# The silu of the MLP's gate goes to the gate's PSUM banks, and the product reads it there

## The chip, the cores and the metric

The kernel runs on one core of a Trainium2 chip. The metric is the device time of one execution in microseconds (us), the median over the runs. Engines are named as in the profile: PE is TensorE (PEld its weight loads), DVE is VectorE, ACT is ScalarE, POOL is GpSimd, SP is the queue that issues most transfers.

## The reference

One layer of a hybrid decoder on 1024 tokens of width 1024, in float32. After a mixer of three head groups comes the gated MLP, and the change lies in its first half:

```python
def conv_gated_mlp(x, w_up, conv_w, w_down):
    h = causal_dwconv(x @ w_up, conv_w)       # 3 taps over the tokens, per channel
    gt, val = jnp.split(h, 2, axis=-1)        # 2 x 2816 channels
    return (jax.nn.silu(gt) * val) @ w_down
```

## The kernel before

The up stage works on 22 tiles j of 128 gate channels and the 128 value channels that belong to them; tokens lie along the free axis, 1024 columns of float32. Each weight and each activation is split in a high and a low half (`slab_p`, `slab_q`; the high one on ScalarE, L2080, the low one on GpSimd, L2087, in a ring of five), and both are multiplied.

Tiles 0 to 2 are done in the plain way, 3 and 4 in four groups of matmuls (A1, A2, B1, B2), and 5 to 21 in seven products of half size, a scheme of Strassen's kind. Each of the seven is a group of eight matmuls (L2263) named by a number i. TensorE's order is 5, 6, 2, 7 of tile j, 1 of tile j+1, then 4 and 3 of tile j. The groups need sums of weights, which VectorE makes ahead (`weight_sum`, L2210; "s" in the written order), copies of some products in SBUF (`copied`, ScalarE, L2144; "k"), and adds of these copies to other products in PSUM (`added`, VectorE, L2217; "a").

A tile's gate and value take two PSUM banks each (`c_ps(0, j)` and `c_ps(1, j)`), and tiles of the same parity share their four banks. When a tile's products are complete, ScalarE writes the convolution's last tap from PSUM to an SBUF buffer (`tapped`, L2102; "t"), and VectorE adds the two other taps to it, reading PSUM again (`tap_one`, L2165, "c"; `tap_zero`, L2171, "v"). For the gate, g = 0, the buffer is `y_a`, one for all tiles; for the value, g = 1, it is `y_b[j % 2]`. ScalarE applies silu to `y_a` in place (L2136; "y"), and VectorE multiplies `y_a` into `y_b` (`prod`, L2227; "p"). The product goes out to memory (`spill`) and is read back in the down stage.

TensorE's groups 5 and 2 write the gate's banks and wait, before the change, for the gate's last tap of tile j-2 (`conv_done(pe, 0, j - 2)`); group 1 waits for that of the value.

All engines follow one order written out by hand, `UP_ORDER` (L298 to L328): each takes from it the steps that are its own. A part of it, for three tiles:

```
... a2.11 s5.12 k7.11 v0.10 h5.12 l5.12 a5.11 y10 s6.12 h2.12 s7.12 k1.12 l2.12 h6.12 p10 h7.12 l6.12 t1.11 a3.11 ...
... a2.14 s5.15 k7.14 a5.14 h5.15 v0.13 l5.15 h2.15 k1.15 s6.15 l2.15 y13 s7.15 h6.15 t1.14 p13 l6.15 h7.15 a3.14 ...
... a2.18 k7.18 s5.19 a5.18 h5.19 v0.17 h2.19 l5.19 k1.19 s6.19 y17 l2.19 s7.19 h6.19 t1.18 l6.19 a3.18 p17 ...
```

"p13" is the product of tile 13, "v0.13" the last tap of its gate, "s6.15" the weight sum of group 6 of tile 15, "h" and "l" the high and low halves of a group's weights. VectorE's own steps are a, s, v, c and p.

Of the kernel before, what the change touches and what calls it, by code (L numbers as in the profile page):

```python
# [25 lines left out]
ACT = mybir.ActivationFunctionType  # L26
ALU = mybir.AluOpType
# [24 lines left out]
NF = DFF // P  # L52
# [220 lines left out]
CLASSIC = 3  # L273
# [141 lines left out]
def build(nc, a, out, scratch, qkv_mid, act_mid, decay_mid, tri_mid, inv_mid, invt_mid):  # L415
    ctx = ExitStack()
    with ctx:
# [7 lines left out]
        def late(name, value=0):  # L425

            early, base = LATE[name]
            return sem(early), base + value
# [315 lines left out]
        y_a = R.view(19456, [S])  # L744
        y_b = [R.view(w, [S]) for w in (27648, 26624)]
        c_ps = lambda g, j: psum[:, 4 * (j % 2) + 2 - 2 * g:4 * (j % 2) + 4 - 2 * g, :].rearrange("p a b -> p (a b)")
# [1222 lines left out]
        def prod_done(eng, j):  # L1969
            eng.wait_ge(*late("up_prod", PRODS.index((j,)) + 1))  # L1970
# [4 lines left out]
        def conv_done(eng, g, j):  # L1975
            eng.wait_ge(*late("up_conv", CONVS.index((g, j)) + 1))
# [112 lines left out]
        def y_of(g, j):  # L2089
            if j < CLASSIC:  # L2090
                return act_f[j] if g else y_up[(j + 1) % 2]
            return y_b[j % 2] if g else y_a

        def conv_source(g, j):
            return up_ps[j % 2][:, g] if j < CLASSIC else c_ps(g, j)

        def up_act(act):
            for s in range(2):
                act.wait_ge(sem(f"x1_st{s}"), 16 * NT // 2)

            def tapped(g, j):
                act.activation(y_of(g, j), conv_source(g, j), ACT.Copy, scale=tap(2, 2 * j + g)).then_inc(late("up_tap")[0], 1)  # L2102

            def tap_(g, j):
                if j < CLASSIC:
                    act.wait_ge(*late("up_mm", 2 * j + g + 1))
                elif j in SEVEN:
                    for i in ((2, 3), (5,))[g]:
                        add_done(act, i, j)
                    mult_done(act, (3, 4)[g], j)  # L2110
                else:
                    mult_done(act, (A2, B2)[g], j)
                if g == 0 and (j == 2 or j >= CLASSIC):
                    prod_done(act, j - 1 if j >= CLASSIC else j - 2)
                elif g == 1 and j >= CLASSIC + 2:
                    spilled(act, j - 2)
                elif g == 1 and j >= CLASSIC:
                    t_ready(act, 7)
                    t_ready(act, 4)
                tapped(g, j)  # L2120

            def t_hi(i):
                t_made(act, "S", i)
                if i == 6:
                    act.wait_ge(*late("up_mm", 1))
                if i == 7:
                    t_ready(act, 4)
                    t_ready(act, 6)
                if i == 4:
                    act.wait_ge(*late("up_mm", 2 * CLASSIC))  # L2130
                    prod_done(act, 1)
                act.activation(t_p[i], t_f[i], ACT.Copy, scale=SPLIT_W).then_inc(late("t_hi")[0], 1)

            def silu(j):
                conv_done(act, 0, j)
                act.activation(y_of(0, j), y_of(0, j), ACT.Silu).then_inc(late("up_silu")[0], 1)  # L2136

            def copied(i, j):

                mult_done(act, i, j)  # L2140
                before = max((x for x in SEVEN if x < j), default=None)
                if before is not None:
                    add_done(act, {1: 2, 6: 3, 7: 5}[i], before)
                act.activation(u_s[i], mult_ps(i, j), ACT.Copy).then_inc(late("c_cp")[0], 1)  # L2144

            up_run(dict(U=lambda u: up_split_hi(act, u), h=lambda i, j: split_mult_hi(act, i, j), k=copied, t=tap_, y=silu, H=t_hi,
                        f=lambda kk: dn_split_hi(act, kk), i=lambda kk: act_split_hi(act, kk)))

# [11 lines left out]
        def up_dve(v):  # L2160

            def tap_one(g, j):
                u, c, y = 2 * j + g, conv_source(g, j), y_of(g, j)
                v.wait_ge(*late("up_tap", TAPS_UP.index((g, j)) + 1))
                v.scalar_tensor_tensor(out=y[:, 1:S], in0=c[:, 0:S - 1], scalar=tap(1, u), in1=y[:, 1:S],  # L2165
                                       op0=ALU.mult, op1=ALU.add).then_inc(late("up_c1")[0], 1)

            def tap_zero(g, j):
                u, c, y = 2 * j + g, conv_source(g, j), y_of(g, j)
                v.wait_ge(*late("up_c1", TAPS_ONE.index((g, j)) + 1))  # L2170
                v.scalar_tensor_tensor(out=y[:, 2:S], in0=c[:, 0:S - 2], scalar=tap(0, u), in1=y[:, 2:S],  # L2171
                                       op0=ALU.mult, op1=ALU.add).then_inc(late("up_conv")[0], 1)

            T_FROM = {5: (0, 0), 7: (0, 1), 6: (1, 1), 4: (1, 0)}

            def whole(i):
                if i in (6, 4):
                    v.wait_ge(*late("up_mm", 2))
                v.scalar_tensor_tensor(out=t_f[i], in0=x_quad(h2_p, *T_FROM[i]), scalar=1.0 / SPLIT_W - 1.0, in1=x_quad(h2_q, *T_FROM[i]),
                                       op0=ALU.mult, op1=ALU.add).then_inc(late("t_f")[0], 1)  # L2180

            def t_sum(i):
                x, y = {5: (7, 5), 7: (6, 7), 6: (6, 5), 4: (4, 6)}[i]
                for z in (x, y):
                    t_made(v, "W", z)
                if i != 5:
                    t_made(v, "S", {7: 5, 6: 7, 4: 6}[i])
                v.tensor_tensor(t_f[i], t_f[x], t_f[y], ALU.subtract).then_inc(late("t_f")[0], 1)

            def t_lo(i):  # L2190
                v.wait_ge(*late("t_hi", T_HIS.index((i,)) + 1))
                v.scalar_tensor_tensor(out=t_q[i], in0=t_p[i], scalar=1.0 - 1.0 / SPLIT_W, in1=t_f[i], op0=ALU.mult, op1=ALU.add)                    .then_inc(late("t_lo")[0], 1)

            def weight_sum(i, j):
                if i == 5:
                    pair_landed(v, j)
                    if seven_before(j) is not None:
                        part_done(v, 3, seven_before(j))
                    out, x, y, op = s_e1[j % 2], w_of(j, 1, 0), w_of(j, 1, 1), ALU.add
                elif i == 6:  # L2200
                    sum_done(v, 5, j)
                    out, x, y, op = s_e2[j % 2], s_e1[j % 2], w_of(j, 0, 0), ALU.subtract
                elif i == 7:
                    sum_done(v, 5, j)
                    out, x, y, op = w_of(j, 1, 0), w_of(j, 0, 0), w_of(j, 1, 0), ALU.subtract
                else:
                    sum_done(v, 6, j)
                    part_done(v, 5, j)
                    out, x, y, op = s_e1[j % 2], w_of(j, 0, 1), s_e2[j % 2], ALU.subtract
                v.tensor_tensor(out, x, y, op).then_inc(late("s_add")[0], 1)  # L2210

            def added(i, j):

                mult_done(v, i, j)
                copy_done(v, {2: 1, 5: 7, 3: 6}[i], j)
                out = c_ps(1, j)[:, right] if i == 5 else mult_ps(i, j)
                v.tensor_tensor(out, mult_ps(i, j), u_s[{2: 1, 5: 7, 3: 6}[i]], ALU.add).then_inc(late("c_add")[0], 1)  # L2217

            def prod(j):
                if j < CLASSIC:  # L2220
                    return
                if j == CLASSIC:
                    for x in range(CLASSIC):
                        prod_done(v, x)
                v.wait_ge(*late("up_silu", SILUS.index((j,)) + 1))
                conv_done(v, 1, j)
                v.tensor_tensor(y_b[j % 2], y_a, y_b[j % 2], ALU.mult).then_inc(late("up_prod")[0], 1)  # L2227

            v.wait_ge(*late("wo_mm", NT))
            v.wait_ge(*late("v_tp", NT))  # L2230
            for s in range(2):
                v.wait_ge(sem(f"x1_st{s}"), 16 * NT // 2)
            v.wait_ge(*late("v_lo", NT))
            up_run(dict(W=whole, S=t_sum, T=t_lo, s=weight_sum, a=added, c=tap_one, v=tap_zero, p=prod, j=lambda kk: act_split_lo(v, kk)))

        def up_pe(pe):
# [7 lines left out]
            for n, (i, j) in enumerate(MULTS):  # L2244
# [1 line left out]
                if i in (1, B1):  # L2246
                    conv_done(pe, 1, j - 2)
                if i in (2, 5, A1):
                    conv_done(pe, 0, j - 2)
                if j < CLASSIC + 2 and i in (1, 2, 5, A1, B1):  # L2250
                    conv_done(pe, 1, j - 2)
                if i in t_p:
# [879 lines left out]
```

## Time and profile before

| what | us |
|---|---|
| median of 3 runs | 1063.14 |
| lowest and highest run | 1062.17, 1066.04 |
| span of the profiled execution | 1063.3 |
| TensorE busy in it | 1025.7 (96%) |
| VectorE busy in it | 813.6 (77%) |
| ScalarE busy in it | 635.0 (60%) |
| GpSimd busy in it | 501.6 (47%) |

The span runs from the first to the last instruction of the profiled execution; it lies 0.2 us above the median of the timed runs. The up stage's groups of seven run from 673.3 to about 892 us of it, the down stage from there to the end. The granted TensorE clock is 1.00 of full speed through both, but for the very end.

### The profile page before, as it was taken

Reading aid. Unit: us, or ns where it says so; the run is one execution under the profiler, and the core shown is the slowest. Engines: PE = TensorE matmul, PEld = TensorE weight load, DVE = VectorE, ACT = ScalarE, POOL = GpSimd, SP = SyncE. Lnnn points to the kernel's source line nnn. Section 1 sums busy time; section 2 is a strip of 40 time slices with the busy share of each in tenths; the row PEclk is TensorE's granted clock in tenths of the full one; section 3 lists DMA queues with packets and bytes.
Section 4 is the critical chain, followed back from the end, with each engine's and each line's share of the span. In section 5 each row is a group of like instructions: output and inputs, shape, how many; then the busy total and the mean of one; then the engine's idle time right before and its main releaser. Section 6 shows DMA issues by size and latency. Waiting matters only on the chain.

```text
span 1063.3 us, 19006 instructions
## 1 busy us (share of the span) xinstructions
PE 1025.7 (96%) x7090; PEld 833.7 (78%) x7090; DVE 813.6 (77%) x1140; ACT 635.0 (60%) x1201; POOL 501.6 (47%) x653
## 2 busy tenths in 40 slices
PE   4999999998999999999999999999999998999997
PEld 4978878986777778777688787888887786888885
DVE  5798895755667886877577598899899999656755
ACT  6634423347777766777865454666666667546443
POOL 2356424725453654542320277788788886000000
PEclk9999999996999999999999999999999999999999
DMA  9245311352122122112263612233443335955961
GB/s 276 68 119 178 110 57 27 70 125 58 41 60 59 27 53 49 29 30 60 80 209 136 198 53 80 79 119 122 127 127 123 123 115 192 382 178 180 334 239 79
DMA packets 159522, 126.77 MB, mean 119 GB/s; under 512 B 63908, under 2 KB 137928, under 8 KB 159432
## 3 DMA queue, kind: packets, MB, share of 16 engines
q1 hardware_dynamic: 157992, 120.32, 37.7%
q10 hardware_dynamic: 1440, 5.24, 1.2%
q8 instruction: 57, 0.93, 0.4%
q14 instruction: 33, 0.27, 0.1%
HBM read 99.79 MB, written 25.71 MB: 118 GB/s over the span
## 4 chain that ended last, share of the span: by engine, by line
PE 60%; DVE 7%; POOL 4%; ACT 3%; issue 3%; DMA 0%; DVEq 0%; ACTq 0%; POOLq 0%
PE psum L2475 14%; PE psum L2263 12%; PE psum L1771 5%; PE psum L1720 5%; PE psum L1704 4%; POOL slab_q L2087 4%; PE psum L1546 4%; PE psum L1689 3%; PE psum L1886 3%; PE psum L2269 2%; DVE arena L2171 1%; DVE arena L2165 1%; PE psum L1625 1%; PE psum L1605 1%; ACT arena L1219 1%
## 5 line engine op out<-in xcount | busy, mean ns | idle before, releaser
L2087 POOL TENSOR_TENSOR slab_q<-arena,slab_p 128x512 fp32r<-128x512 f32 x127 | 208.2, 1667 | 45.5 <-ACT slab_p L2080 45.4
L2475 PE MATMUL psum<-dn_p,ap_p 128*128 128x512 f32 x352 | 110.2, 392 | 2.7 <-DVE arena L2171 1.4
L2475 PE MATMUL psum<-dn_q,ap_q 128*128 128x512 f32 x352 | 109.7, 391 | 0.0
L2263 PE MATMUL psum<-t_p,slab_p 128*128 128x512 f32 x272 | 106.3, 391 | 1.3 <-ACT arena L2144 0.8
L2263 PE MATMUL psum<-t_q,slab_q 128*128 128x512 f32 x272 | 105.9, 389 | 0.0
L2080 ACT ACTIVATE slab_p<-arena 128x512 fp32r<-128x512 f32 x127 | 78.2, 627 | 38.7 <-PE psum L2263 13.9
L2301 DVE TENSOR_TENSOR dn_q<-arena,dn_p 128x1024 fp32r<-128x1024 f32 x41 | 50.2, 1224 | 56.3 <-ACT dn_p L2291 56.0
L1431 DVE CUSTOM_DVE_ANT_0 psum<-psum,arena 128x640 f32<-128x640 f32 (+7 forms) x96 | 67.7, 718 | 31.2 <-PE psum L1689 30.6
L2291 ACT ACTIVATE dn_p<-arena 128x1024 fp32r<-128x1024 f32 x44 | 46.6, 1058 | 70.0 <-PE psum L2475 63.6
L3051 PE MATMUL psum<-h_p,cm_p 128*128 128x512 f32 (+1 forms) x288 | 87.5, 375 | 0.6 <-DVE arena L2958 0.6
L3051 PE MATMUL psum<-h_q,cm_q 128*128 128x512 f32 (+1 forms) x288 | 86.9, 373 | 0.0
L2263 PE MATMUL psum<-h_p,slab_p 128*128 128x512 f32 x204 | 79.9, 391 | 0.7 <-POOL slab_q L2087 0.7
L2475 PEld LDWEIGHTS psum<-dn_p,ap_p 128*128 128x128 f32 x352 | 65.7, 188 | 18.8 <-issue 2.5
L1219 ACT ACTIVATE arena<-psum,arena 128x640 f32<-128x640 f32 (+7 forms) x96 | 67.1, 702 | 21.1 <-DVE arena L1431 20.3
L2263 PE MATMUL psum<-h_q,slab_q 128*128 128x512 f32 x204 | 79.4, 389 | 0.0
L2466 POOL TENSOR_TENSOR arena<-arena 128x1024 f32<-128x1024 f32 x1 | 2.4, 2352 | 160.6 <-DVE arena L2439 160.6
L2475 PEld LDWEIGHTS psum<-dn_q,ap_q 128*128 128x128 f32 x352 | 66.1, 188 | 14.5
L2936 DVE SCALAR_TENSOR_TENSOR arena<-psum,arena 128x1023 f32<-128x1023 f32 (+29 forms) x60 | 75.9, 1265 | 1.4
L1226 ACT ACTIVATE arena<-psum 128x384 f32<-128x384 f32 x132 | 60.1, 488 | 23.3 <-PE psum L1704 22.1
L2210 DVE TENSOR_TENSOR arena<-arena 128x512 f32<-128x512 f32 x68 | 72.6, 1082 | 0.0
L2576 POOL TENSOR_TENSOR cm_q<-arena,cm_p 128x1024 fp32r<-128x1024 f32 x16 | 39.2, 2449 | 61.8 <-ACT cm_p L2571 61.7
L1720 PE MATMUL psum<-arena 128*64 128x192 f32 x528 | 64.2, 348 | 1.4 <-ACT arena L1226 1.4
(319 smaller groups left out, 2636.4 us busy)
## 6 DMA issues: line engine op xcount, KB each, us to landing
arena<-in_ffn_w_up SPq DMA_DIRECT2D x44, 512.0 KB, 4.9
arena<-in_ffn_w_down SPq DMA_DIRECT2D x44, 512.0 KB, 3.9
arena<-in_w_in SPq DMA_DIRECT2D x20, 512.0 KB, 3.9
act_mid<-arena SPq DMA_DIRECT2D x18, 512.0 KB, 2.6
arena<-act_mid SPq DMA_DIRECT2D x36, 256.0 KB, 4.7
arena<-in_x SPq DMA_DIRECT2D x16, 512.0 KB, 4.6
qkv_mid<-arena ACTq DMA_DIRECT2D x9, 512.0 KB
arena<-qkv_mid SPq DMA_DIRECT2D x8, 576.0 KB, 4.9
```

The costliest lines, as they stand in the source:

```text
L1219: act.activation(probs(u), s_psum(u, n), ACT.Exp, scale=-1.0, bias=nmx[:, u % 2:u % 2 + 1], accum_out=psums[:, NH * kind + h:NH * kind + h ...
L1226: act.activation(pt[x % 2].rearrange("p g c -> p (g c)"), psum[:, bank, 0:GDIM], ACT.Copy).then_inc(done, 1)
L1431: v.tensor_tensor_reduce(out=s_psum(u, n), in0=s_psum(u, n), in1=hidden, scale=-1.0, scalar=-NEG, op0=ALU.add, op1=ALU.min, accum_out=nmx[ ...
L1720: ins = pe.matmul(psum[tok, 7, 0:GDIM // 2], val[:, b, kind, HD * kv:HD * (kv + 1)], pt[x % 2][:, :, tok], start=b == k0, stop=True, skip_ ...
L1771: ins = pe.matmul(wm_ps[WM_SLOT[t]][:, n * 512:(n + 1) * 512], x[:, k], w[:, n * 512:(n + 1) * 512], start=first and k == ks[0] and w is w ...
L2080: act.activation(slab_p[n % RING], part_source(i, j), ACT.Copy, scale=1.0 - SPLIT_W).then_inc(late("up_hi")[0], 1)
L2087: pool.tensor_tensor(slab_q[n % RING], part_source(i, j), slab_p[n % RING], ALU.subtract).then_inc(late("up_lo")[0], 1)
L2210: v.tensor_tensor(out, x, y, op).then_inc(late("s_add")[0], 1)
L2263: ins = pe.matmul(mult_ps(i, j), w[:, k], x[:, k], start=k == 0 and x is x_p[i] and i in (1, 2, 5), stop=True, skip_group_check=True)
L2475: ins = pe.matmul(dn_ps[t % HT][:, n * 512:(n + 1) * 512], x[:, tok], w[:, n * 512:(n + 1) * 512], start=first and x is ap_p[s], stop=True ...
L2936: own.up(v.scalar_tensor_tensor(out=cacc[:, c, s:S], in0=glu[c][:, 0:S - s], scalar=w, in1=cacc[:, c, s:S], op0=ALU.mult, op1=ALU.add))
L3051: ins = pe.matmul(cm_ps[i % 2][:, c0:c1], w[:, k], x[:, k, c0:c1], start=k == 0 and x is h_p, stop=True, skip_group_check=True)
```

## The change

For tiles 3 to 19 silu is written to the gate's PSUM banks, whose sums have been read for the last time by then; the product takes its first operand there. `y_a` is then free as soon as silu has read it, so ScalarE's next tap into it waits for silu instead of the product. The gate's banks are free only when the product has read them, so TensorE's groups 5 and 2 of tile j wait for the product of tile j-2. Tiles 20 and 21 keep silu in `y_a`. `UP_ORDER` is as before.

```diff
+        def gate_of(j):
+            return c_ps(0, j) if CLASSIC <= j < NF - 2 else y_of(0, j)
+        def silu_done(eng, j):
+            eng.wait_ge(*late("up_silu", SILUS.index((j,)) + 1))
+        def bank_free(eng, j):
+            if CLASSIC <= j < NF - 2:
+                prod_done(eng, j)
+            else:
+                conv_done(eng, 0, j)
...
-                if g == 0 and (j == 2 or j >= CLASSIC):
+                if g == 0 and CLASSIC < j < NF - 1:
+                    silu_done(act, j - 1)
+                elif g == 0 and (j == 2 or j >= CLASSIC):
                     prod_done(act, j - 1 if j >= CLASSIC else j - 2)
...
             def silu(j):
                 conv_done(act, 0, j)
-                act.activation(y_of(0, j), y_of(0, j), ACT.Silu).then_inc(late("up_silu")[0], 1)
+                act.activation(gate_of(j), y_of(0, j), ACT.Silu).then_inc(late("up_silu")[0], 1)
...
-                v.tensor_tensor(y_b[j % 2], y_a, y_b[j % 2], ALU.mult).then_inc(late("up_prod")[0], 1)
+                v.tensor_tensor(y_b[j % 2], gate_of(j), y_b[j % 2], ALU.mult).then_inc(late("up_prod")[0], 1)
...
                 if i in (2, 5, A1):
-                    conv_done(pe, 0, j - 2)
+                    bank_free(pe, j - 2)
```

CLASSIC is 3 and NF is 22.

## Rows read from the trace of the kernel before

**Rows 1.** The page: each engine's busy time, share of the span, instructions.

```profile
PE 1025.7 (96%) x7090; PEld 833.7 (78%) x7090; DVE 813.6 (77%) x1140; ACT 635.0 (60%) x1201; POOL 501.6 (47%) x653
```

**Rows 2.** Stretches: length, busy time of each engine, granted clock, DMA share, GB/s.

```profile
core 0: us, PE busy (x) PEld busy (x) DVE busy (x) ACT busy (x) POOL busy (x), PEclk, DMA share, GB/s
...
762.50:853.90 91.40, 90.46 (x393) 73.07 (x393) 91.25 (x84) 61.34 (x92) 76.91 (x50) 1.00 0.39 121
```

**Rows 3.** Waits from 640 to 905 us: total, times, longest.

```profile
PEld psum L2263 <- POOL slab_q L2087: 4.5, 9, 0.6
```

**Rows 4.** Timeline of TensorE: start and length in us, first matmuls of groups.

```profile
673.30 0.39 PE L2263 MATMUL psum<-t_p,slab_p 128*128 128x512 f32 x1
...
685.99 0.39 PE L2263 MATMUL psum<-t_p,slab_p 128*128 128x512 f32 x1
...
788.55 0.39 PE L2263 MATMUL psum<-t_p,slab_p 128*128 128x512 f32 x1
...
795.80 0.44 PE L2263 MATMUL psum<-h_p,slab_p 128*128 128x512 f32 x1
...
801.31 0.39 PE L2263 MATMUL psum<-t_p,slab_p 128*128 128x512 f32 x1
...
853.90 0.39 PE L2263 MATMUL psum<-t_p,slab_p 128*128 128x512 f32 x1
```

**Rows 5.** Timeline of VectorE: start and length in us, idle time before in brackets.

```profile
672.84 1.28 DVE L2165 SCALAR_TENSOR_TENSOR arena<-psum,arena 128x1023 f32<-128x1023 f32 x1 [2.94 <-ACT arena L2102]
674.04 1.75 DVE L2227 TENSOR_TENSOR arena<-arena 128x1024 f32<-128x1024 f32 x1
...
683.51 2.31 DVE L2227 TENSOR_TENSOR arena<-arena 128x1024 f32<-128x1024 f32 x1
...
787.98 2.31 DVE L2227 TENSOR_TENSOR arena<-arena 128x1024 f32<-128x1024 f32 x1
...
796.75 0.69 DVE L2217 TENSOR_TENSOR psum<-psum,arena 128x512 f32<-128x512 f32 x1
797.35 1.27 DVE L2171 SCALAR_TENSOR_TENSOR arena<-psum,arena 128x1022 f32<-128x1022 f32 x1
798.54 2.64 DVE L2210 TENSOR_TENSOR arena<-arena 128x512 f32<-128x512 f32 x2
801.10 2.33 DVE L2227 TENSOR_TENSOR arena<-arena 128x1024 f32<-128x1024 f32 x1
...
854.11 0.70 DVE L2217 TENSOR_TENSOR psum<-psum,arena 128x512 f32<-128x512 f32 x1 [0.35 <-PE psum L2263]
854.71 1.28 DVE L2227 TENSOR_TENSOR arena<-arena 128x1024 f32<-128x1024 f32 x1
```

**Rows 6.** Single lines of VectorE: durations min/median/max in ns, first and last start.

```profile
L2227 DVE TENSOR_TENSOR arena<-arena x19: 1209/1746/2328, 674.0 to 900.4; 128x1024 f32<-128x1024 f32 x19
L2210 DVE TENSOR_TENSOR arena<-arena x68: 671/934/1842, 662.2 to 883.5; 128x512 f32<-128x512 f32 x68
L2165 DVE SCALAR_TENSOR_TENSOR arena<-psum,arena x44: 1266/1271/1285, 613.6 to 896.6; 128x1023 f32<-128x1023 f32 x44
L2217 DVE TENSOR_TENSOR psum<-psum,arena x51: 680/686/700, 679.4 to 893.5; 128x512 f32<-128x512 f32 x51
```

**Rows 7.** Timeline at the start of the down stage: VectorE, then TensorE.

```profile
895.44 1.28 DVE L2171 SCALAR_TENSOR_TENSOR arena<-psum,arena 128x1022 f32<-128x1022 f32 x1
...
896.87 0.70 PE L2475 MATMUL psum<-dn_p,ap_p 128*128 128x512 f32 x2 [1.02 <-DVE arena L2171]
```

**Rows 8.** Timeline of ScalarE: the copy of group 7 and silu in one tile.

```profile
796.00 0.60 ACT L2144 ACTIVATE arena<-psum 128x512 f32<-128x512 f32 x1 [2.03 <-PE psum L2263]
...
798.89 1.05 ACT L2136 ACTIVATE arena<-arena 128x1024 f32<-128x1024 f32 x1
```

**Rows 9.** Groups of ScalarE by form: busy us, mean ns of one.

```profile
L2792 ACT ACTIVATE psum<-psum 128x1024 f32<-128x1024 f32 x2 | 2.0, 1008 | 4.5 <-PE psum L3051 4.5
```

**Rows 10.** Stretches of the down stage, columns as in the second group.

```profile
891.70:920.00 28.30, 25.96 (x110) 20.16 (x109) 19.98 (x20) 13.21 (x16) 4.17 (x2) 1.00 0.89 329
920.00:960.00 40.00, 40.00 (x176) 32.83 (x175) 21.42 (x24) 18.97 (x24) 0.00 (x0) 1.00 0.68 240
```

## The prediction

> **What bounds the kernel now.** I read the page first. TensorE is busy in nearly the whole span, VectorE in three quarters of it [rows 1]; that is an average over stages, so the next view is the table of stretches around the change. In the middle of the up stage, from 762.5 to 853.9 us, TensorE has work 90.46 of 91.40 us and VectorE 91.25 of 91.40 [rows 2]. Two engines are full there at once, and VectorE is the one without reserve. The table of waits says what this costs TensorE: 4.5 us in nine waits for GpSimd's low halves, in which the longest is 0.6 us [rows 3].
>
> TensorE's own pace comes from the timeline. Call group (i, j) the eight matmuls of product i of tile j; the order is 5, 6, 2, 7, then 1 of the next tile, 4, 3. Group (5,14) starts at 788.55 and group (1,15), four groups later, at 795.80 [rows 4]: 1.81 us a group, 12.69 us for seven. From (5,5) at 673.30 to (5,19) at 853.90 are 14 tiles in 180.60 us [rows 4]; at 12.69 they would take 177.66. All waiting in that stretch is 2.9 us. This is the most that any relief of the other engines can give back there.
>
> **The change part by part.** *The new gate.* Group (5, j) overwrites the gate's right half of tile j-2. It used to wait for the last convolution tap of that gate; now it waits for the product of tile j-2, for j from 5 to 21: 17 gates. Group (2, j) gets the same wait and finds it met, since it comes two groups later. Behind (5, j) stands the whole TensorE queue, so each late product is a hole in the bounding engine. The question is where the product ends against the start of (5, j), which the VectorE timeline tells [rows 5].
>
> *The product itself.* Now it takes 1.21 to 2.33 us, median 1.75, for one and the same shape [rows 6]. What varies with it is the other instruction with both operands in SBUF, the weight sums at 671 to 1842 ns; instructions with one operand in PSUM keep one duration: the tap at 1266 to 1285 ns over 44, the add of half the length at 680 to 700 over 51 [rows 6], while GpSimd works beside them. The product with its gate in PSUM is of this second kind, so I take 1.23 us (twice the add less one fixed part: the bounds are its own 1.21 and the tap's 1.28, and 2.33 if the place of the operand did not matter; the nearest rows speak for the low end). Its end reaches TensorE after 0.15 us: a convolution ends at 895.44 + 1.28 = 896.72 and the matmul that waited for it starts at 896.87 [rows 7]. So a gate opens 1.38 us after the product starts.
>
> The Trainium skill ("VectorE: DVE Perf Modes", section on the TRN2 errata) speaks a little against this: it gives VectorE 62 cycles more for a PSUM source than for SBUF, by its 0.96 GHz an estimated 65 ns. The trace agrees in sign and not in size: the fastest SBUF sum of 512 columns takes 671 ns, the PSUM add 680 to 700 [rows 6]. By the page the stalls below would total about 0.5 us more.
>
> *First gate, (5,5).* The product of tile 3 starts at 674.04 behind a tap that waited for ScalarE until 672.84 [rows 5]; that tap needs tile 4's last group, so the order can't move. It opens at 675.42, group (5,5) started at 673.30 [rows 4]: a hole of 2.1 us.
>
> *Gates (5,6) to (5,11).* Here the product ends before the group begins. The tightest of the six is (5,6): the product ran from 683.51 for 2.31 us, to 685.82 [rows 5], and the group began at 685.99 [rows 4]; with 1.23 us it opens 1.1 us ahead. Nothing.
>
> *Gates (5,12) to (5,18).* These are the tiles in which VectorE never rests. For (5,14) the product starts at 787.98 [rows 5], opens at 789.36, the group started at 788.55 [rows 4]: 0.8 us. For (5,15): 801.10 and 802.48 against 801.31: 1.2 us. Of the seven, three have VectorE's order of (5,14) (0.8, 0, 0.8) and four that of (5,15) (1.2 each): 6.3 us if everything ahead of the product stays as it is. It does stay for a part: the chain from group 7 is paced by TensorE. Group 7 ends about 795.8, ScalarE's copy runs 796.00 to 796.60 [rows 8], the add at 796.75 is 8.20 us behind the start of (5,14), then the last tap, the two sums (2.64 us together) and the product [rows 5]. Relief of VectorE earlier in the tile cannot move that. What can move is the contention of the two sums: at 0.67 each the product would start at 8.20 + 0.60 + 1.19 + 1.2 = 11.2 us, but silu ends at 798.89 + 1.05 = 799.94, which is 11.39 [rows 8], so the gate opens at 12.8 us against 12.69: a hole of 0.1, and 0.6 us for all seven. Between 0.6 and 6.3 I take 4.0, nearer to the contended end, since the high half that ScalarE makes next after the copy sets GpSimd to work in just that part of the tile.
>
> *Gates (5,19) to (5,21).* In the written order the add of group 3 now stands ahead of the product (a3.18 p17, and so on). Group 3 of tile j-1 is the one right before (5, j) on TensorE. So the product cannot start before TensorE has run dry: the add started at 854.11, 0.21 behind (5,19), the product at 854.71 [rows 5], it would open at 856.09 against 853.90 [rows 4]. That is 2.2 us, three times: 6.6.
>
> *What is given back.* Holes let GpSimd fill its five slabs, and VectorE has up to 1.1 us less per tile: the 2.9 us of waits go, all but a little; I take 2.7.
>
> *The rest costs nothing.* Silu into PSUM: it takes 1.05 us from SBUF to SBUF [rows 8], and the one ScalarE instruction that writes 1024 columns of PSUM takes 1008 ns [rows 9]; ScalarE idles two fifths of the span, and uncovered it would cost the 0.1 us once per late gate at most. The gate's first tap on ScalarE waits for silu instead of the product: earlier, and not on TensorE's path. The last two tiles keep the old places, so the down stage's banks come free as before. Nor does it absorb the delay: it begins with 25.96 busy of 28.30 us, then 40.00 of 40.00 [rows 10], so at most some 2 us of its first waits could.
>
> The sum: 2.1 + 4.0 + 6.6 - 2.7 = +10.0 us on the profiled span of 1063.3, which is 0.2 above the median of the runs, 1063.14. So 1073 us; with 0.6 or 6.3 in the middle and 2.9 or 1.5 given back, 1069.5 to 1076.6.
>
> **The rivals.**
> *VectorE's relief decides (not slower).* VectorE paces tiles 10 to 16, at (853.90 - 801.31)/4 = 13.15 us a tile [rows 4]; 1.1 us less per product lets TensorE run at 12.69, and the product lands ahead of its gate. All holes away, it is 1063.3 - 2.9 = 1060.4. The point from which it decides: the product must start 11.3 us after (5, j-1). For: six gates already do so. Against: silu's end at 11.39, and the order at the last three. If only the middle holes vanish it is +5.8 or so, at the edge of what can be told; with some of it absorbed in the down stage it is within the noise.
>
> *The sums get worse.* GpSimd and the two sums block one another in turn: at 1.84 us each [rows 6] the product opens 2.4 us late four times and 1.2 us three times, 12.9 instead of 4.0: 1082. For: TensorE's holes shift GpSimd's work against VectorE's. Against: only a few sums reach that now. The Trainium skill ("SBUF — State Buffer", section Who interferes with whom) says that who starts first holds the shared port for the whole instruction, which would make this chance of phase all or nothing; the spread in [rows 6] agrees, and no run here shows which phase will come.
>
> *The product is no faster.* If the operand's place doesn't matter it keeps 2.33: 2.6 for the first gate, 1.1 more at each of seven, 3.3 at each of three; 2.6 + 11.7 + 9.9 - 2.7 gives 1085. Against it stand 95 PSUM instructions of one duration.
>
> **How the numbers follow.** A measurement of this kernel tells about 0.5%, 5.3 us, from no change. The forecast of +6 to +14 gets 0.68; worse sums 0.12; a product no faster 0.05; relief that eats most of the holes 0.15, of which 0.12 lies within 0.5% and 0.03 below it. So slower 0.85, same 0.12, faster 0.03. The range 1066 to 1080 leaves out the lower part of the relief case, the upper part of the worse sums and the product no faster: under 2 in 10.
>
> **What the profile would show.** Right: the product at 1.21 to 1.29 us throughout; TensorE waiting for VectorE's product line ahead of group 5, about 2.1 us at the first of these tiles and in the last three, under 1.3 in between, none in tiles 6 to 11; the waits for GpSimd's slabs nearly gone; VectorE with idle time between 762 and 854. Wrong: product durations still between 1.2 and 2.3; no wait ahead of (5,19) to (5,21); holes in tiles 6 to 11 too (contention moved there), or a down stage that starts 10 us later and ends less than 8 us later.

## The result and the profile after

The changed kernel takes 1081.17 us in the median (1079.93 to 1083.26, four runs) against 1063.33 beside it: 1.0165 times as long, with a 95% interval of 1.0149 to 1.0182, or 17.8 us. The forecast was slower, by 10; the range ended at 1080.

First the page of the changed kernel, each engine's busy time, as [rows 1].

```profile
PE 1029.1 (95%) x7090; PEld 834.5 (77%) x7090; DVE 799.4 (74%) x1140; ACT 633.7 (59%) x1201; POOL 479.0 (44%) x653
```

VectorE and GpSimd are busy for less time than before, and the kernel is slower. The stretch of [rows 2] shows the same in the middle of the up stage: VectorE was full and now rests 8.3 of 91.4 us; TensorE rested 0.9 and now rests 4.6.

```profile
core 0: us, PE busy (x) PEld busy (x) DVE busy (x) ACT busy (x) POOL busy (x), PEclk, DMA share, GB/s
762.50:853.90 91.40, 86.79 (x377) 69.80 (x376) 83.10 (x81) 56.28 (x86) 65.24 (x48) 1.00 0.37 116
```

The lines of the product, of silu and of the weight sums in the changed kernel, durations as in [rows 6] (L2243 was L2227, L2152 was L2136, L2226 was L2210):

```profile
L2243 DVE TENSOR_TENSOR arena<-psum,arena x17: 1208/1214/1218, 673.5 to 893.5; 128x1024 f32<-128x1024 f32 x17
...
L2152 ACT ACTIVATE psum<-arena x17: 1010/1022/1024, 668.1 to 890.3; 128x1024 f32<-128x1024 f32 x17
L2152 ACT ACTIVATE arena<-arena x5: 1043/1059/1066, 622.5 to 916.0; 128x1024 f32<-128x1024 f32 x5
...
L2226 DVE TENSOR_TENSOR arena<-arena x68: 678/746/1793, 661.7 to 895.8; 128x512 f32<-128x512 f32 x68
```

The 17 products with an operand in PSUM all take 1.21 us, where the same work took up to 2.33; silu is 0.04 us shorter into PSUM than into SBUF. Both instructions got cheaper, and the weight sums too in the median (746 ns against 934).

Why the product got shorter can be read beside GpSimd's timeline. The first two lines are of the kernel before, around its product of 801.10 to 803.43 us [rows 5]; the other two of the changed kernel, around a product of 845.01 to 846.22:

```profile
800.60 1.75 POOL L2087 TENSOR_TENSOR slab_q<-arena,slab_p 128x512 fp32r<-128x512 f32 x1
802.31 2.27 POOL L2087 TENSOR_TENSOR slab_q<-arena,slab_p 128x512 fp32r<-128x512 f32 x1
...
844.67 1.56 POOL L2087 TENSOR_TENSOR slab_q<-arena,slab_p 128x512 fp32r<-128x512 f32 x1
846.20 1.29 POOL L2087 TENSOR_TENSOR slab_q<-arena,slab_p 128x512 fp32r<-128x512 f32 x1
```

With both operands in SBUF the product ended 1.08 us behind the GpSimd instruction that was running when it began, and the next GpSimd instruction ended 1.15 us behind the product: they went one after the other. All nine products of 2.31 to 2.33 us before began beside a running GpSimd instruction like this; the eight of 1.21 to 1.28 began with GpSimd idle or within 0.2 us of the start or end of one of its instructions. With one operand in PSUM they run side by side: the product of 845.01 takes its 1.21 us beside a running GpSimd instruction, and one that began with the product of 748.39 took 1.31 us, where before one that began with the product of 747.13 took 2.36.

What the change cost stands in TensorE's timeline, ahead of group 5: of tile 5, of tile 18 and of tile 19 here.

```profile
670.97 0.39 PE L2279 MATMUL psum<-h_p,slab_p 128*128 128x512 f32 x1
...
672.56 0.39 PE L2279 MATMUL psum<-h_q,slab_q 128*128 128x512 f32 x1
674.84 0.47 PE L2279 MATMUL psum<-t_p,slab_p 128*128 128x512 f32 x1 [1.89 <-POOL slab_q L2087]
...
845.21 0.39 PE L2279 MATMUL psum<-h_q,slab_q 128*128 128x512 f32 x1
846.32 0.47 PE L2279 MATMUL psum<-t_p,slab_p 128*128 128x512 f32 x1 [0.72 <-POOL slab_q L2087]
...
858.88 0.39 PE L2279 MATMUL psum<-h_q,slab_q 128*128 128x512 f32 x1
861.23 0.47 PE L2279 MATMUL psum<-t_p,slab_p 128*128 128x512 f32 x1 [1.96 <-POOL slab_q L2087]
861.54 0.39 PE L2279 MATMUL psum<-t_q,slab_q 128*128 128x512 f32 x1
...
862.24 0.63 PE L2279 MATMUL psum<-t_p,slab_p 128*128 128x512 f32 x1
862.66 0.63 PE L2279 MATMUL psum<-t_q,slab_q 128*128 128x512 f32 x1
...
908.25 0.39 PE L2279 MATMUL psum<-h_q,slab_q 128*128 128x512 f32 x1
```

Matmuls start 0.227 us apart when nothing waits; what goes beyond that ahead of group 5 is the hole: 2.05 us, 0.88 and 2.12 here. The table of waits from 640 to 905 us puts them down to GpSimd:

```profile
PEld psum L2279 <- POOL slab_q L2087: 17.2, 11, 2.9
...
PE psum L2279 <- POOL slab_q L2087: 12.9, 11, 2.5
```

It is not GpSimd. Group 5 waits for its slab and for the product; there are eleven holes, as many as gates that the prediction priced, and the VectorE timeline has a product that ends 0.10 us ahead of each:

```profile
673.52 1.22 DVE L2243 TENSOR_TENSOR arena<-psum,arena 128x1024 f32<-128x1024 f32 x1
...
840.90 0.70 DVE L2233 TENSOR_TENSOR psum<-psum,arena 128x512 f32<-128x512 f32 x1 [0.80 <-ACT arena L2160]
841.50 1.27 DVE L2187 SCALAR_TENSOR_TENSOR arena<-psum,arena 128x1022 f32<-128x1022 f32 x1
842.69 2.39 DVE L2226 TENSOR_TENSOR arena<-arena 128x512 f32<-128x512 f32 x2
845.01 1.21 DVE L2243 TENSOR_TENSOR arena<-psum,arena 128x1024 f32<-128x1024 f32 x1
...
859.30 0.70 DVE L2233 TENSOR_TENSOR psum<-psum,arena 128x512 f32<-128x512 f32 x1 [0.55 <-PE psum L2279]
859.91 1.21 DVE L2243 TENSOR_TENSOR arena<-psum,arena 128x1024 f32<-128x1024 f32 x1
```

674.74, 846.22 and 861.12 are the ends; 674.84, 846.32 and 861.23 the starts of group 5. In tile 18 the product comes behind the add that waits for ScalarE's copy, the tap and two sums of 2.39 us together; in tile 19 behind the add that waits for TensorE.

And there is something the prediction does not have. Behind the hole at 861 the matmuls soon start 0.43 us apart instead of 0.227. The stretches of one microsecond there, and two each behind the holes ahead of (5,20) and (5,21), columns as above:

```profile
861.00:862.00 1.00, 0.77 (x4) 0.68 (x5) 1.00 (x2) 0.00 (x0) 1.00 (x2) 1.00 0.03 12
862.00:863.00 1.00, 1.00 (x4) 0.84 (x3) 0.94 (x2) 0.00 (x0) 0.38 (x1) 0.59 1.01 410
863.00:864.00 1.00, 1.00 (x4) 0.71 (x3) 0.00 (x0) 0.00 (x0) 0.00 (x0) 0.50 0.26 102
864.00:865.00 1.00, 1.00 (x4) 0.81 (x3) 0.00 (x0) 0.82 (x2) 0.11 (x1) 0.50 0.00 0
865.00:866.00 1.00, 1.00 (x4) 0.78 (x4) 0.15 (x1) 0.82 (x1) 1.00 (x1) 0.70 0.00 0
...
880.00:881.00 1.00, 1.00 (x4) 0.76 (x3) 0.00 (x0) 0.70 (x2) 0.00 (x0) 0.50 0.00 0
881.00:882.00 1.00, 1.00 (x4) 0.81 (x3) 0.04 (x1) 0.93 (x1) 1.00 (x1) 0.50 0.00 0
...
897.00:898.00 1.00, 1.00 (x4) 0.74 (x3) 1.00 (x2) 0.00 (x0) 0.00 (x0) 0.50 0.00 0
898.00:899.00 1.00, 1.00 (x4) 0.81 (x3) 0.37 (x1) 0.00 (x0) 0.00 (x0) 0.50 0.00 0
```

The granted clock is 0.50 there, the lower of its two levels (1.2 of 2.4 GHz). PE counts as fully busy all the while, so busy time does not show it; only the clock column and the count of matmuls do. It happens behind each of the three late holes, and costs 1.7 us each time (the lengths of groups 5 and 6 against 1.81 us).

To compare kernels without what lies ahead of the change, I take the stretch from the first matmul of group (1,5) to the start of the last matmul of (3,21): 891.47 - 671.49 = 219.98 us before, 908.25 - 670.97 = 237.28 after, 17.3 more. The start of that stretch moves between 668.8 and 673.6 us from profile to profile, although the edits hardly touch what lies ahead of it; what follows it takes 171.8 us in all but one of them (the relief of VectorE alone, below).

### The profile page after: what moved, and what is told of

Its sections match the earlier page's. It is cut to its first block, busy times and chain, and to the rows that moved or that the text cites. A ratio compares the mean times of both kernels' runs of the same rounds, so it can differ in the third digit from the quotient of the medians.

```text
span 1080.1 us, 19006 instructions
## 1 busy us (share of the span) xinstructions
PE 1029.1 (95%) x7090; PEld 834.5 (77%) x7090; DVE 799.4 (74%) x1140; ACT 633.7 (59%) x1201; POOL 479.0 (44%) x653
## 4 chain that ended last, share of the span: by engine, by line
PE 62%; POOL 5%; ACT 4%; DVE 4%; issue 3%; DMA 2%; DVEq 0%; SPq 0%; ACTq 0%; POOLq 0%
PE psum L2279 17%; PE psum L2491 14%; PE psum L1720 4%; PE psum L1704 4%; PE psum L1771 4%; POOL slab_q L2087 3%; PE psum L1546 3%; PE psum L1886 3%; PE psum L1689 2%; PE psum L2285 2%; ACT arena L1219 1%; PE psum L1625 1%; PE psum L1605 1%; ACT slab_p L2080 1%; PE psum L1493 1%
## 5 line engine op out<-in xcount | busy, mean ns | idle before, releaser
L2087 POOL TENSOR_TENSOR slab_q<-arena,slab_p 128x512 fp32r<-128x512 f32 x127 | 185.5, 1475 | 85.0 <-ACT slab_p L2080 83.6
L2279 PE MATMUL psum<-t_p,slab_p 128*128 128x512 f32 x272 | 109.8, 404 | 13.7 <-POOL slab_q L2087 12.9
L2279 PE MATMUL psum<-t_q,slab_q 128*128 128x512 f32 x272 | 108.8, 400 | 0.0
L2279 PEld LDWEIGHTS psum<-t_p,slab_p 128*128 128x128 f32 x272 | 52.8, 194 | 29.4 <-POOL slab_q L2087 17.2
L2181 DVE SCALAR_TENSOR_TENSOR arena<-psum,arena 128x1023 f32<-128x1023 f32 x44 | 55.9, 1274 | 18.4 <-ACT arena L2116 18.4
L2226 DVE TENSOR_TENSOR arena<-arena 128x512 f32<-128x512 f32 x68 | 68.7, 1026 | 0.0
```

Source lines behind the costliest of these rows:

```text
L2087: pool.tensor_tensor(slab_q[n % RING], part_source(i, j), slab_p[n % RING], ALU.subtract).then_inc(late("up_lo")[0], 1)
L2279: ins = pe.matmul(mult_ps(i, j), w[:, k], x[:, k], start=k == 0 and x is x_p[i] and i in (1, 2, 5), stop=True, skip_group_check=True)
```

## The experiments

My theory was now: holes ahead of group 5, and a halved clock behind the longest of them. "The stretch" below is the one just defined.

**The early gates alone.** The three places where the range of tiles stands get 3 <= j < 17.

```diff
-            return c_ps(0, j) if CLASSIC <= j < NF - 2 else y_of(0, j)
+            return c_ps(0, j) if 3 <= j < 17 else y_of(0, j)
```

> The change for tiles 3 to 16 alone; tiles 17 to 19 keep silu in SBUF and the old gate. My theory: the three late gates cost about 12 us (holes of 2.1 to 2.7 us and, behind each, 1.7 us lost to a TensorE clock at half its rate), so what is left is the first hole (2.1) and seven holes of 0.8 to 1.0 (6.4) less 3.3 given back: about +5, 1068 us, and no stretch with a granted clock near 0.5 in the up stage. Rival: the late gates cost only their holes, as predicted (6.6), and the rest is spread: about 1074. Rival: the slow stretches do not belong to the late gates: they stay or move into tiles 17 to 21, 1073 or more.

1071.37 us (1.0065 times before, 1.0049 to 1.0081); the stretch takes 227.68 us, 7.7 more than before. The late holes and their slow stretches are gone, the seven middle holes are those of the changed kernel (0.72 to 0.89 us). But the clock fell behind the first hole, which it had not done in the profile of the changed kernel; that is 1.6 of the 3.4 us by which my 1068 is short. The hole is the same 2.05 us in both.

**The late gates alone.** The same places with 17 <= j < 20.

> The change for tiles 17 to 19 alone. My theory: three holes of 2.1 to 2.7 us and the halved clock behind each: about +12, 1075 us, the waits of the middle tiles as in the kernel before. Rival: a hole costs its own length: +6.6, 1070 us. Rival: the clock falls only because the tiles before had holes too (an accumulated effect): granted clock 1.00 here, 1070 us.

1074.5 us (1.0099, 1.0076 to 1.0121); the stretch is 11.7 us longer. Three holes (2.12, 2.12, 2.66 us) and the lower clock behind each; no gate before them had a hole, so the fall does not need earlier ones. A hole priced by its length, 6.6 us, is not enough.

**TensorE kept at work in the late holes.**

```diff
+                if i == 5 and j >= 19:
+                    t_ready(pe, i)
+                    for k in range(HT):
+                        for w, x in ((slab_p[n % RING], x_p[i]), (slab_q[n % RING], x_q[i])):
+                            pe.matmul(c_ps(1, j)[:, right], w[:, k], x[:, k], start=True, stop=True, skip_group_check=True)
                 if i in (2, 5, A1):
                     bank_free(pe, j - 2)
```

> The changed kernel with eight extra matmuls in each of the three late holes: TensorE runs group 5's own eight products once more, into the free right bank of the value, ahead of the wait for the product. They take 1.8 us, less than the hole. My theory: the clock falls because TensorE stands still; with the filler the granted clock stays at 1.00 behind these holes, the holes themselves stay as long: about 5 us less than the changed kernel, 1076 us, although TensorE does more. Rival: the slow matmuls have another cause (the transfers or the PSUM traffic of these tiles): no gain, 1081 us, or a loss.

The stretch shrinks by 3.3 us against the changed kernel, to 234.02. The time, 1079.35 us, is nearer to the rival's 1081 than to 1076, but the late part of the profile did what the theory says. These are stretches at and behind two of the late gates; the clock stays at 1.00:

```profile
864.00:867.00 3.00, 2.90 (x13) 2.33 (x13) 2.00 (x3) 0.64 (x2) 1.46 (x2) 1.00 0.43 175
867.00:870.00 3.00, 3.00 (x15) 2.48 (x14) 1.97 (x2) 2.12 (x3) 1.93 (x2) 1.00 0.04 12
...
894.00:897.00 3.00, 2.85 (x13) 2.00 (x12) 3.00 (x4) 1.32 (x2) 2.47 (x2) 1.00 0.43 175
897.00:900.00 3.00, 3.00 (x15) 2.49 (x14) 1.21 (x2) 1.46 (x3) 0.26 (x1) 1.00 0.00 0
```

The holes are as long as they were (2.07, 2.08 and 2.62 us from group to group), and 24 matmuls more make the late tiles 4.9 us shorter. In this profile the clock fell behind the first hole, which took 1.6 back.

The filler also settles what group 5 waits for. The first extra matmul of the hole ahead of (5,19) and, eight matmuls on, group 5 itself:

```profile
862.14 0.39 PE L2268 MATMUL psum<-t_p,slab_p 128*128 128x512 f32 x1
...
864.22 0.50 PE L2284 MATMUL psum<-t_p,slab_p 128*128 128x512 f32 x1
```

The extra matmuls read both halves of group 5's own weights and start without a wait, so GpSimd's slab was ready; group 5 still waited, for the product.

**And in the first hole.** The condition becomes `j == 5 or j >= 19`.

> As the filler in the three late holes, and the same eight extra matmuls in the first hole, ahead of group 5 of tile 5, too. In the traces so far the clock fell behind the first hole in three of the four kernels that have it with its 2.05 us, and not in the profile of the changed kernel, so the time with the late filler alone was mixed. My theory: now the clock stays at 1.00 behind all four: 1081.2 less 5.1 and less 1.3 (three quarters of 1.7) is 1074.8 us, with little spread. Rival: the small gain of the late filler in time (1.8 us in the median) is all there is to have, 1078 to 1080 us, because the extra matmuls cost what the clock gives back.

The stretch takes 232.43 us, 4.9 less than in the changed kernel, and the clock is at 1.00 behind all four gates. That is what the three slow stretches cost (5.1), but for 0.2; the changed kernel's profile has none behind the first hole. The time, 1077.0 us, lies between theory and rival: 11.9 us above the kernel before beside it, where the changed kernel was 17.8 above. The other runs say the same: the mean granted clock of the whole execution is 0.989 to 0.992 in the four runs of this kernel, 0.983 to 0.988 in the four of the changed kernel, and 0.991 to 0.997 in the seven of the kernel before beside this one.

**The late products ahead of the add.** In the written order `a3.18 p17` becomes `p17 a3.18`, and the same for tiles 18 and 19.

> The changed kernel with the products of tiles 17, 18 and 19 written ahead of the add of group 3 instead of behind it, as it is for the tiles before. My theory: the three late holes shrink to the size of the middle ones, 0.8 to 1.0 us, too short for the clock to fall: 12 us become about 3, so 1072 us. Rival: the add comes 1.1 us later and holds back the next tile's taps and sums, which makes another wait: 1076 or more. Rival: clock falls in these tiles whatever the hole: 1077.

1075.98 us, 4 above my 1072; the stretch is 4.7 us shorter than in the changed kernel. For (5,19) and (5,20) as expected: holes of 0.88 us, clock 1.00. Not for (5,21), whose hole is still 2.06 us (2.66 in the changed kernel) with the clock down behind it: in that tile's order the sum of group 5 stands between the add and the tap, the two sums behind the tap took 2.96 us together, and the product started 13.5 us behind (5,20) instead of 12.4. The clock fell behind the first hole too, which cost 1.6. Stretches behind (5,19) and (5,21):

```profile
863.00:866.00 3.00, 3.00 (x15) 2.48 (x14) 2.21 (x3) 2.12 (x3) 1.95 (x2) 1.00 0.05 16
888.00:891.00 3.00, 2.23 (x7) 1.81 (x8) 3.00 (x4) 2.17 (x3) 3.00 (x3) 0.78 0.44 178
```

**The middle products between the two sums.** In the written order `s7.15 ... p13` becomes `p13 s7.15`, for tiles 10 to 16.

> The changed kernel with only the products of tiles 10 to 16 written between the two weight sums, the rest as in the change. My theory: the sums, 2.4 us together beside GpSimd, made the middle holes of 0.8 to 1.0; with one sum less ahead, the product waits for silu alone and the hole is 0.1 or none: about 5.6 us less, 1075.5 us, first and late holes as they are. Rival: the weight sum that now comes 1.2 us later makes GpSimd late and TensorE waits for the slab of group 7 instead: 1080 us.

1075.85 us (1.0102, 1.0082 to 1.0122), stretch 230.12. The seven holes are gone but for 0.1 us of a longer first matmul in five of them; in those five the product now waits for silu (0.45 to 0.85 us), as the prediction's lower end had it. One wait for a slab of 0.4 us appeared at (1,15). So the two sums ahead of the product made the middle term. The clock fell behind the first hole and at the 2.66 us hole of (5,21), but not behind the two holes of 2.12 us at (5,19) and (5,20):

```profile
858.00:861.00 3.00, 2.21 (x10) 1.86 (x11) 2.50 (x3) 0.09 (x1) 1.95 (x2) 1.00 0.43 175
861.00:864.00 3.00, 3.00 (x15) 2.49 (x14) 1.42 (x2) 2.67 (x4) 1.38 (x2) 1.00 0.00 1
...
889.00:892.00 3.00, 2.82 (x7) 2.27 (x8) 3.00 (x4) 0.88 (x1) 1.95 (x2) 0.50 0.43 175
```

**The new gate alone, product in SBUF.**

```diff
         def gate_of(j):
-            return c_ps(0, j) if CLASSIC <= j < NF - 2 else y_of(0, j)
+            return y_of(0, j)
```

with the old wait of the gate's tap for the product.

> The kernel before with the new gate alone: silu and product stay in SBUF, but TensorE's groups 5 and 2 wait for the product all the same. My theory: the product keeps up to 2.3 us, so every hole is about 1.1 us longer than in the changed kernel: the seven middle ones reach 2 us, long enough for the clock to fall behind them too. First hole 2.6, middle 7 x 2.0 and up to 7 x 1.7 for the clock, late 3 x (3.3 + 1.7): 1093 to 1105 us. Rival: the operand's place in PSUM does not matter for the product's time: the same as the changed kernel, 1081 us. Rival: the clock does not fall in the middle: about 1093 at most.

1096.35 us (1.0319, 1.0295 to 1.0343). The product's line in it:

```profile
L2241 DVE TENSOR_TENSOR arena<-arena x19: 1210/2290/2326, 674.3 to 936.3; 128x1024 f32<-128x1024 f32 x19
```

The first hole is 2.55 us, the middle ones are 1.82 to 1.98, the late ones 3.1 to 3.2. The clock fell behind the first and the late ones, behind three of the four of 1.97 and 1.98 us, and behind none of the three shorter ones (in the longest of the four runs, 1100.97 us, which is the profiled one). So the place in PSUM saved some 15 us of what the gate alone costs.

**Relief of VectorE alone.**

```diff
-                v.tensor_tensor(y_b[j % 2], y_a, y_b[j % 2], ALU.mult)
+                v.tensor_tensor(y_b[j % 2][:, left], y_a[:, left], y_b[j % 2][:, left], ALU.mult)
```

> The kernel before with the product on the left half of the columns only (the right half of the activations stays without its gate), so that VectorE has some 0.6 to 1.1 us less per tile and no new wait exists. My theory: all that relief of VectorE can give is the 3.3 us of waits for GpSimd's slabs: 1060 to 1063 us. Rival: VectorE's queue is the bound of the middle tiles and its relief is worth 1.1 us a tile over 16 tiles: 1046 us.

1058.67 us (0.9953, 0.9939 to 0.9966), a little below the theory's 1060 and far from the rival's 1046; the stretch takes 217.1 us, 2.9 less than before, and all its tiles but one take the free 12.69 us: a lighter VectorE can give hardly more in the stretch. Another 2.1 of the 5.7 us comes behind it, where 169.7 us are left instead of 171.8: this experiment halves the products of the last two tiles too, and TensorE's first waits for VectorE in the down stage shrink from 2.7 to 1.0 us. The change leaves those two in SBUF, so that part is not within its reach.

**The change with an order that fits it.** For tiles 10 to 18, in the written order:

```diff
-a2.14 s5.15 k7.14 a5.14 h5.15 v0.13 l5.15 h2.15 k1.15 s6.15 l2.15 y13 s7.15 h6.15 t1.14 p13 l6.15 h7.15 a3.14
+a2.14 s5.15 v0.13 k7.14 a5.14 h5.15 y13 l5.15 h2.15 k1.15 s6.15 p13 l2.15 s7.15 h6.15 t1.14 l6.15 h7.15 a3.14
```

Tile 19 likewise (`a2.20 v0.19 e0 a5.20 y19` and `s6.21 p19`), and `p3` ahead of `c1.4`.

> The changed kernel with VectorE's order fitted to the new gate: from tile 10 on the gate's last tap goes ahead of the add of group 5, its silu ahead of ScalarE's next high half, and the product between the two weight sums and ahead of the add of group 3; the product of tile 3 goes ahead of the value's tap of tile 4. My theory: the product then starts about 9.8 us after group 5 of the tile and opens the gate 1.5 us before it is needed; no hole, no fall of the clock, and the 3.3 us of waits stay given back: 1060 us. Rival: the weight sums, now behind the product, are late for GpSimd and put the waits back: 1063 to 1066 us.

1061.59 us against 1064.36 beside it: 0.9983 (0.9972 to 0.9993). The stretch takes 217.19 us, 2.8 less than before and 20.1 less than in the changed kernel. No hole is left at a gate but 0.4 us at (5,21), where the kernel before has 0.3. The VectorE timeline at tile 16: the product ends at 809.14, and TensorE starts group (5,16) at 810.21.

```profile
806.57 1.44 DVE L2225 TENSOR_TENSOR arena<-arena 128x512 f32<-128x512 f32 x1
807.93 1.21 DVE L2242 TENSOR_TENSOR arena<-psum,arena 128x1024 f32<-128x1024 f32 x1
809.07 0.67 DVE L2225 TENSOR_TENSOR arena<-arena 128x512 f32<-128x512 f32 x1
```

```profile
810.21 0.39 PE L2278 MATMUL psum<-t_p,slab_p 128*128 128x512 f32 x1
```

**That order in the kernel before.**

> The kernel before with that same order, silu and product in SBUF and the old gate: what the order alone does. My theory: nothing waits for the product here, so the order alone moves little: the products still take up to 2.3 us and VectorE stays full, 1061 to 1064 us. Rival: the order alone takes the waits away: 1060 us, and the place in PSUM is worth nothing.

1065.41 us (1.0018, 1.0007 to 1.0030); the stretch takes 221.61 us, 1.6 more than before: TensorE loses 1.3 us in tile 12, some 0.6 in each of tiles 13 to 15 and 0.2 in each of 16 to 19, mostly to waits for slabs. So the order is worth nothing without the short product, and the change nothing without the order. Together they are slightly ahead of both kernels, by about as much as the relief alone gives in the stretch.

## Why the prediction failed, step by step

What the stretch shows against the terms of the sum, in us. The first matmul behind a hole takes some 0.1 us longer than the others; that is counted with the holes of the first and the middle gates, and for the last three it lies in the clock's row:

| term | predicted | measured |
|---|---|---|
| first gate, (5,5) | 2.1 | 2.2 |
| gates (5,6) to (5,11) | 0 | 0 |
| gates (5,12) to (5,18) | 4.0 (0.6 to 6.3) | 6.4 |
| gates (5,19) to (5,21), holes | 6.6 | 6.9 |
| the clock behind them | not priced | 5.1 |
| waits given back | -2.7 | -3.3 |
| sum | +10.0 | +17.3 |

**The failed step is that of gates (5,19) to (5,21).** The order argument held for the first two: the product came behind the add, the add behind TensorE, and the holes are 2.12 us each. At (5,21) the add waited for two sums of 2.96 us, the hole is 2.66, and with the product ahead of the add it was still 2.06: there VectorE's own queue was as late as TensorE, and a hole of about 2.2 was partly luck. But the step failed elsewhere: each hole was priced at its length, as if the matmuls behind it ran as before. Some eight of them ran at the lower clock, which cost 1.7 us each time. The late gates alone showed it without the other holes, and the filler took it away by adding work; had transfers or PSUM traffic made the matmuls slow, they would have stayed slow. Over all profiles the clock fell at 19 of the 23 unfilled holes of 1.97 us or more, and at none of the seven filled ones (2.01 to 2.62 us). Without these 5.1 us the time would have been about 1076, inside the range; the kernel with all four long holes filled measured 1077.0.

**Mis-sized: the middle.** The mechanism and the places were right, the seven holes are there, but the two sums took 2.39 us in four of these tiles and 3.43 in the other three, where one alone takes 0.68 when nothing holds it up. I had expected GpSimd's work to move out of their way in part, and it did not. The upper end, 6.3, was the better estimate, but that it fits so well is partly luck: the holes themselves are 0.73 us three times and 0.88 four times, 5.7 in all, against 0.8, 0, 0.8 and 1.2 four times, and the other 0.7 is the longer first matmul behind each, which the sum did not have. Moving one sum behind the product removed the term.

**Right:** the product's 1.21 us and its cause (17 instructions of one duration; with both operands in SBUF and the same gate they went back to 2.29 in the median), the first hole, the six gates without any, the relief worth 3 us in the stretch (and 3.3 given back), the cheap silu, and a down stage that absorbs nothing (171.8 us before and after). The section on who interferes with whom of the Trainium skill's page "SBUF — State Buffer" says that a VectorE instruction with at most one SBUF input does not contend with GpSimd; these 17 products, at 1208 to 1218 ns beside a GpSimd that works, agree.

**Wrong, though the 2.1 us came true:** that the order can't move at the first gate. The product of tile 3 does not need the tap that it stood behind; in the fitted order it goes ahead of it, starts 3.3 us ahead of group (5,5), and that hole is gone.

**Open:** when exactly the clock falls. In the profiles with the new gate and without a filler in the hole, it fell at none of the 40 gate holes of 0.7 to 1.83 us, at all seven of 2.5 us or more, and at 12 of the 16 of 1.97 to 2.12 us, with the same hole at the same gate ending both ways in different profiles. Length alone does not decide it. That the time shows 17.8 us and the stretch 17.3 is no finding: the part ahead of the stretch differs by more than that from profile to profile.

## What to carry to other kernels

When a buffer's release moves from one instruction to a later one on another engine, find in the written order what stands between the two, and whether any of it waits for the engine that wants the buffer: that can make a hole in each round, however short the later instruction gets. Price a hole in a full TensorE by its length and by the matmuls at half clock that may follow. Here the cheaper instruction paid for the later release only with the order rewritten so that the release comes early in its round.

## What was not expected of the hardware

After TensorE had stood still for 2.12 us in a stream of dense matmuls, the granted clock went from 1.00 to 0.50 not at once but about 1 us after it had started again: up to 862.24 the matmuls start at about the old distance (0.23 to 0.31 us), from there on 0.43 us apart. The delay is not fixed: behind (5,20) and (5,21) of the same profile it is 1.5 us, and in the profile with the middle products moved the clock fell in the hole of (5,21) itself, so that the first two matmuls already start 0.56 us apart. The Trainium skill ("TensorE: Matmul & The Clock Gate", Part 1) has the clock depend on recent activity, with these two levels, which the trace bears out. And a multiplication that does the same work on the same 1024 columns took 1.21 us with one operand in PSUM, always, and 1.21 to 2.33 with both in SBUF, by what GpSimd was doing when it began: beside a busy GpSimd, PSUM was the faster place to read from.
